# A layer with two attention stages: the softmax weighing moved to GpSimd alone, and the output projection's first weights loaded ahead

## The reference, cut to what matters

```
h = u @ w_in
o_nsa = nsa_mixer(q_a, ...)         # 8 heads of 64 in 2 groups: three branches, each softmax weighed by a gate
o_mla = mla_mixer(cq, ckv, k_rope)  # 8 heads of 96/64 on rms-normed latents of rank 384 and 256, causal over all keys
y = concatenate([o_nsa, o_mla]) @ w_out
x = layer_norm(ALPHA * x + (1 + g2) * y)
p = e / max(sum(e), 1e-30)          # in every softmax; e are the exponentials
```

## Time and profile before

| what | us |
|---|---|
| median of three runs (lowest, highest) | 2243.52 (2240.02, 2244.45) |
| the profiled execution, own time | 2248.16 |
| its span, first to last instruction | 2246.2 |
| PE, DVE, ACT, POOL busy in the span | 2093.4, 1543.6, 992.7, 707.0 |
| mean granted TensorE clock | 0.965 of full speed |

### The profile page before, as it was taken

The page is one execution under the profiler, slowest core; times in us unless marked ns, Lnnn a source line. Parts: engine busy times, 40 slices in busy tenths (PEclk is TensorE's granted clock), DMA queues, the critical chain, the costliest instruction groups (busy, mean ns, idle before and its releaser), DMA issues. The chain is left out here.

```text
span 2246.2 us, 28288 instructions
## 1 busy us (share of the span) xinstructions
PE 2093.4 (93%) x10025; PEld 1749.0 (78%) x10025; DVE 1543.6 (69%) x2387; ACT 992.7 (44%) x1901; POOL 707.0 (31%) x657
## 2 busy tenths in 40 slices
PE   6999999999999999788998889889899999999997
PEld 4888888878887887777786877767788888887885
DVE  6777777766887314798887487853765555558689
ACT  3433333334554123777876456530833333324443
POOL 0366555511100001255451032300245565640301
PEclk9999999999998999799998989989999999999999
DMA  7245555468831311300000000040333333247975
GB/s 266 94 162 168 169 169 169 159 206 261 244 105 62 123 45 43 87 1 1 1 1 1 1 1 1 1 145 18 133 117 104 112 106 120 93 125 264 295 258 100
DMA packets 193633, 254.39 MB, mean 113 GB/s; under 512 B 18192, under 2 KB 116560, under 8 KB 193495
## 3 DMA queue, kind: packets, MB, share of 16 engines
q1 hardware_dynamic: 178088, 208.04, 27.9%
q0 software_dynamic: 15408, 44.57, 7.6%
HBM read 212.72 MB, written 43.52 MB: 114 GB/s over the span
## 5 line engine op out<-in xcount | busy, mean ns | idle before, releaser
L2856 POOL TENSOR_TENSOR nsa_exps<-nsa_exps,nsaa_factor 128x512 f32<-128x512 f32 (+1 forms) x96 | 90.4, 972 | 120.5 <-DVE nsaa_factor L2836 120.5
L749 DVE TENSOR_TENSOR ffn2A_u<-ffn2A_u,ffn_banks 128x512 f32<-128x512 f32 x60 | 41.2, 687 | 117.4 <-PE ffn_banks L693 117.4
L1283 DVE SCALAR_TENSOR_TENSOR late_part_late<-ada_rows,far_silu_c,late_part_late 128x1024 f32<-128x1024 f32 x56 | 106.7, 1906 | 5.3 <-DMA ada_rows<-in_w_ada 5.3
L570 ACT ACTIVATE ffn1A_t_hi<-ffn1A_t 128x512 fp32r<-128x512 f32 x80 | 48.5, 628 | 132.6 <-POOL ffn1A_t L563 101.7
L570 ACT ACTIVATE ffn2A_t_hi<-ffn2A_t 128x512 fp32r<-128x512 f32 x80 | 48.4, 628 | 122.2 <-POOL ffn2A_t L563 91.3
L2783 ACT ACTIVATE nsaa_turned_hi<-nsaa_ring 128x512 fp32r<-128x512 f32 (+1 forms) x148 | 85.3, 599 | 35.0 <-PE nsaa_ring L2744 24.8
L2026 PE MATMUL in_acc<-mix_in_w_hi,mix_in_u_hi 128*128 128x494 f32 x256 | 99.2, 388 | 0.8 <-PEq L86 0.8
L2026 PE MATMUL in_acc<-mix_in_w_lo,mix_in_u_hi 128*128 128x494 f32 x256 | 99.2, 388 | 0.0
L2026 PE MATMUL in_acc<-mix_in_w_hi,mix_in_u_lo 128*128 128x494 f32 x256 | 99.2, 388 | 0.0
L2823 DVE TENSOR_TENSOR nsaa_turned_lo<-nsaa_ring,nsaa_turned_hi 128x512 fp32r<-128x512 f32 x132 | 87.9, 683 | 14.3 <-ACT nsaa_turned_hi L2783 12.3
L693 PE MATMUL ffn_banks<-ffn1S_s_hi,ffn1A_t_hi 128*128 128x512 f32 x240 | 93.8, 391 | 0.0
(11 more groups left out here) (640 smaller groups left out, 7035.3 us busy)
## 6 DMA issues: line engine op xcount, KB each, us to landing
ada_rows<-in_w_ada POOLq DMA_DIRECT2D x56, 512.0 KB, 4.7
ffn_raw_g<-in_ffn_wg SPq DMA_DIRECT2D x44, 512.0 KB, 3.7
ffn_raw_u<-in_ffn_wu SPq DMA_DIRECT2D x44, 512.0 KB, 5.0
early_w<-in_w_ada SPq DMA_DIRECT2D x16, 512.0 KB, 7.0
mix_in_w_raw<-in_w_in SPq DMA_DIRECT2D x32, 247.0 KB, 2.6
ffn_rest<-in_ffn_wd SPq DMA_DIRECT2D x29, 256.0 KB, 5.4
hidden<-ffn1A_c SPq DMA_DIRECT2D x22, 256.0 KB, 4.6
hidden<-ffn1A_u SPq DMA_DIRECT2D x22, 256.0 KB, 5.0
```

Source lines behind the costliest of these rows:

```text
L570: act.activation(self.b_hi[w][:, :], self.block_of(w), ACT.Copy).then_inc(self.rounded, 1)
L749: dve.tensor_tensor(out, base, bank, ALU.add).then_inc(self.mixed, 1)
L1283: dve.scalar_tensor_tensor(out=part_late[:, v, :], in0=ada[:, n % 2, :], scalar=silu_c[:, k:k + 1], in1=part_late[:, v, :], op0=ALU.mult, ...
L2856: pool.tensor_tensor(at, at, by, ALU.mult).then_inc(weighed_pool, 1)
```

## The change

- Weighing: POOL weighs all blocks in both stages; DVE's weigh step (L2841) is gone. A unit has no `by_vector` any more.
- `scale_latents` is done by POOL, after its last weigh step of each of the first 16 sparse units.
- The plan: `pool_price` falls from 2.9 to 1.67 a column (and 100 to 145 an instruction), with 1100 for a `scale_latents`; DVE's factor step is priced 300 throughout. In the latent stage PE's ranks for scoring, turning, applying change from (2, 0, 1) to (1, 0, 2).
- The output projection's gate row and first four chunks of w_out are asked for by SP inside the latent stage, as soon as PE is done with the last stage step. They go to the places of ukv_lo and ukv_hi; the chunks' high and low parts later go to the places of kv_hi and kv_lo. These four tiles are not read after the last stage step.

```diff
 def pool_price(u, step):
     kind, n, k = step
-    return 100 + (4 - u.weighed_rows(k)) * u.keys * 2.9
+    own = 145 + (4 - u.first_row(u.blocks[k])) * u.keys * 1.67
+    return own + (1100 if u.gate is not None and n < 2 * TT and k == len(u.blocks) - 1 else 0)
...
     streams = {"pe": [scoring, turning, applying], "act": [scores, filled, folding],
-               "dve": [scores, filled, factors, by_vector, folding], "pool": [by_pool]}
+               "dve": [scores, filled, factors, folding], "pool": [weighing]}
...
         @block.sync
         def _(sp):
             if ahead is not None:
                 ahead(sp)
+            if behind is not None:
+
+                sp.wait_ge(ring_full, max(m for x, m in ring_no.items() if x[0] == "stage") + 1)
+                behind(sp)
...
-                    if k < u.by_vector:
-                        pe.wait_ge(weighed_dve, weigh_no["weigh", n, 0] + 1)
-                    else:
-                        pe.wait_ge(weighed_pool, weigh_no["weigh", n, k] + 1)
+                    pe.wait_ge(weighed, weigh_no["weigh", n, k] + 1)
...
-                    if beside is not None:
-                        beside(dve, n)
                     dve.wait_ge(floored, n + 1)
                     dve.reciprocal(factor[:, b, :], floor[:, b, :]).then_inc(factored, 1)
-                elif kind == "weigh":
-                    dve.wait_ge(factored, n + 1)
-                    for r in range(4):
-                        at = u.room[:, r, 0:min(u.widths[r], u.by_vector * u.keys)]
-                        last = dve.tensor_scalar(at, at, factor[:, n % SUMS, r:r + 1], None, ALU.mult)
-                    last.then_inc(weighed_dve, 1)
...
-                pool.tensor_tensor(at, at, by, ALU.mult).then_inc(weighed_pool, 1)
+                pool.tensor_tensor(at, at, by, ALU.mult).then_inc(weighed, 1)
+                if beside is not None and k == len(u.blocks) - 1:
+                    beside(pool, n)
...
-               {"pe": (2, 0, 1), "act": (1, 0, 2), "dve": (2, 1, 0, 0, 3), "pool": (0,)}, 0)
+               {"pe": (1, 0, 2), "act": (1, 0, 2), "dve": (2, 1, 0, 3), "pool": (0,)}, 0, behind=behind)
```

More of the change, by code:

```diff
@@ L1833, in __init__ @@
         if gate_dram is not None:
-            self.gate = s.sb("gate", [P, w_dram.shape[1]])
+            self.gate = places[1] if places else s.sb("gate", [P, w_dram.shape[1]])
             self.gate_in = s.sem("gate_in")
@@ L1925, in load @@
                     chunks.load(sp, n, c)
-            if reload is not None:
-                chunks.ahead(sp)
             load(0, slots)
@@ L2434, in __init__ @@
         self.together = 4 if max(widths) <= T // 4 else 2 if max(widths) <= T // 2 else 1
-        self.by_vector, self.room = by_vector, room
-    def parts_weighed(self):
-        whole = [(0, self.by_vector)] if self.by_vector else []
-        return whole + [(k, k + 1) for k in range(self.by_vector, len(self.blocks))]
-    def weighed_with(self, k):
-        return 0 if k < self.by_vector else k
-    def weighed_rows(self, k):
-        return 0 if k < self.by_vector else self.first_row(self.blocks[k])
+        self.room = room
     def columns(self, row, width=None):
@@ L2527, in dve_price @@
     if kind == "factor":
-        return 300 if u.gate is None or n >= 2 * TT else 520
-    if kind == "weigh":
-        return 4 * (60 + u.by_vector * u.keys * 0.52)
+        return 300
     return (4 - u.first_row(u.blocks[k])) * P * 1.04 + 70 if kind == "turn" else 670
@@ L2557, in plan @@
         factors += [("factor", n, 0)]
-        for k0, k1 in u.parts_weighed():
-            (by_vector if k0 < u.by_vector else by_pool).append(("weigh", n, k0))
+        weighing += [("weigh", n, k) for k in range(len(u.blocks))]
         if u.closes:
@@ L2605, in needs @@
         elif kind == "turn":
-            found.append(("dve" if k < u.by_vector else "pool", ("weigh", n, u.weighed_with(k))))
+            found.append(("pool", ("weigh", n, k)))
         elif kind == "apply":
@@ L2639, in plan, with attend @@
     return order
-def attend(nc, stage, units, staging, folding, ident, ident_r, copies, first, slack, ahead=None, beside=None):
+def attend(nc, stage, units, staging, folding, ident, ident_r, copies, first, slack, ahead=None, beside=None, behind=None):
     order = plan(units, copies, first, slack)
@@ L2962, in sparse_attention, with latent_attention @@
         attend(nc, stage + "a", units, Staging(), Folding(), ident, ident_r, 6,
-               {"pe": (0, 1, 2), "act": (2, 0, 1), "dve": (2, 1, 0, 0, 3), "pool": (0,)}, 0, ahead=ahead, beside=scale_latents)
-def latent_attention(nc, stage, h, kv_hi, kv_lo, ukv_hi, ukv_lo, v, ident, ident_r, causal):
+               {"pe": (0, 1, 2), "act": (2, 0, 1), "dve": (2, 1, 0, 3), "pool": (0,)}, 0, ahead=ahead, beside=scale_latents)
+def latent_attention(nc, stage, h, kv_hi, kv_lo, ukv_hi, ukv_lo, v, ident, ident_r, causal, behind):
     with Scope(nc, stage) as s:
@@ L3030, in unit @@
                         lambda r: [((4 * half + r) * P, causal[:, :])], lambda j: v[:, head, j, :], 2 * head + half, True, True,
-                        None, before, 3, 1360, 3 * half, rooms[2 * b + half])
+                        None, before, 3, 1360, rooms[2 * b + half])
         class Folding:
@@ L3131, in layer @@
                                  compressed, rstd, latent_weights.ahead)
+            with Scope(nc, "out_w") as early:
+                early.sb("base", [P, 4 * T])
+                out_raw, out_gate = early.sb("raw", [P, Chunks.SLOTS, HALF]), early.sb("gate", [P, D])
+            split = h_alive.enter_context(Scope(nc, "split"))
+            kv_hi = split.sb("kv_hi", [P, 2, T], F32R)
+            kv_lo = split.sb("kv_lo", [P, 2, T], F32R)
+            ukv_hi = split.sb("ukv_hi", [P, 2, HEADS * P], F32R)
+            ukv_lo = split.sb("ukv_lo", [P, 2, HEADS * P], F32R)
+            slots_of = lambda at: at[:, :, :].rearrange("p a (b n) -> p (a b) n", n=HALF)
+            places = (out_raw, out_gate, slots_of(kv_hi), slots_of(kv_lo))
+            chunks = Chunks(split, w_out[0], HALF, gate_dram[0:1, :], places=places)
             with Scope(nc, "latent") as b:
[L3133 to L3136 removed]
                 v = b.sb("v", [P, HEADS, TT, P], F32R)
@@ L3143, in layer @@
                 latent_in.__exit__(None, None, None)
-                latent_attention(nc, "mla", h, kv_hi, kv_lo, ukv_hi, ukv_lo, v, ident, ident_r, causal)
+                latent_attention(nc, "mla", h, kv_hi, kv_lo, ukv_hi, ukv_lo, v, ident, ident_r, causal, chunks.ahead)
             clear_semaphores(nc)
@@ L3152, in layer @@
             x_back = r.sem("x_back")
-            chunks_in = Scope(nc, "w_out", side="right")
-            chunks_in.__enter__()
-            chunks = Chunks(chunks_in, w_out[0], HALF, gate_dram[0:1, :])
             heads_out = [COL_Q + c * P for c in range(HEADS // 2)] + LATENT_OUT
```

34 lines of the change are left out of this document (16 added, 18 removed).

## The result

The changed kernel takes 2204.35 us (median of 4 runs, 2200.80 to 2207.36), the kernel before 2243.98 us beside it (4 runs, 2240.02 to 2246.43). The ratio is 0.9824, with a 95% interval of 0.9802 to 0.9847: 39.6 us less. The profiled execution took 2202.52 us with a span of 2200.7 us, 45.6 us less than that of before; the mean granted clock is 0.977 (0.965 before).

A forecast was written before the change was run, and what follows sets the result against it. Latent attention was held bound by a chain of waits, chiefly PE's for DVE's weighing; DVE nearly bound part of the sparse stage. 24.5 + 5.7 + 4.8 = 35.0 us off the median 2243.5 gave 2208.5 us; range 2194 to 2230.

The forecast's parts named there:

- the likeliest case: Whole kernel: a time of 2200 to 2217 us, given a chance of 0.57.
- its largest term: Latent attention: 24.5 us saved, 20.3 over seven intervals between heads and 4.2 at the last half 1.
- The latent chain: Latent attention: PE's waits for DVE's weighing and the clock's falls behind them go; a head takes 20.9 us, not 23.8.
- The sum over heads: Latent attention: seven intervals between eight heads, each 2.9 us shorter, give 20.3 us.
- The last half 1: Latent attention's end: the wait of 5.3 us falls to POOL's 1.1 us, giving 4.2 us.
- The floor and the new waits: Latent attention, per head: PE's own work is the floor at 19.9 us, plus 1.0 us of new waits.
- the ring's turnaround: Latent attention: PE's new order waits for three banks and their copies; 1.3 us a turnaround, up to 2.5 us a head.
- The sparse attention: Sparse stage: 5.7 us from two thirds of DVE's 8.6 us relief, between 0 and 12; nothing for the reordering.
- POOL's scaling: Sparse stage: each scaling on POOL takes 0.8 us, between 0.37 and 1.5, covered by POOL's idle time.
- The projection: Output projection: early loads let PE start at 1474.3, not 1479.08, saving 4.8 us; range 4 to 7.5.
- The page on ports: Sparse stage: a shared SBUF port lets busier POOL hold DVE's small operations, 7 us; hence two thirds of 8.6 us.
- The last rival: Reordering gives nothing and POOL's late latents take the sparse gain: 4.8 us from the projection, 2238 us; chance 0.05.

The follow-up runs named there:

- experiment 1: Kernel before, with POOL weighing every block of the latent attention at its old price and PE's old rank; 2221.24 us, ratio 0.9905.
- Experiment 6: Kernel before, nothing moved, but POOL waits in the latent attention until DVE has weighed its blocks; 2213.01 us, ratio 0.9866.
- Experiment 2: Changed kernel with PE's rank in the latent attention as before, (2, 0, 1); 2211.36 us, ratio 0.9869.
- experiment 7: Kernel before with only PE's ranks in the latent attention changed to (1, 0, 2); 2244.62 us, ratio 1.0005.
- 8: Changed kernel, but its latent attention has the division, prices and rank of before, with POOL weighing behind DVE; 2201.65 us, ratio 0.9804.
- 9: As 8, with the new POOL price and rank (1, 0, 2) in the latent attention and the planner told of POOL's wait; 2200.22 us, ratio 0.9794.
- experiment 3: Changed kernel with the latents scaled by DVE again, prices of DVE and POOL as without it; 2205.41 us, ratio 0.9839.
- experiment 5: Changed kernel with POOL's steps at the old price in both attention stages; 2227.75 us, ratio 0.9926.
- experiment 4: Changed kernel with the gate row and first w_out chunks asked for at the projection again; 2206.68 us, ratio 0.9834.
- experiment 10: As 9, but DVE weighs all of the latent attention and POOL does nothing there; 2231.16 us, ratio 0.9938.

## Why the prediction was right

The forecast was 2208.5 us; 2204.35 was measured, inside both the range and the likeliest case's own. The mechanism of its largest term is the one that the chip shows. That the sum comes so close is in part luck: the two profiled executions lie 45.6 us apart where the steps gave 35.0, and only the medians lie 39.6 apart. By its own steps:

**The latent chain: right, its cause incomplete.** PE's wait for the weighing and the clock's falls behind it are gone, as experiment 1 shows by that edit alone. A head takes 20.7 us in the steady state; 20.9 was forecast. DVE's 15.9 us and POOL's 10.3 us a head were right within a microsecond: in the 20.85 us of one head from 1303.95 on they are busy for 16.7 and 9.5. But the prediction took DVE's 1058 ns as what the operation costs. Experiment 6 puts it at 415 ns: the other 643 ns are POOL's presence. The 4.0 us were a collision, and the change removes it by leaving one party.

**The sum over heads: mis-sized.** "Seven intervals of 2.9, 20.3 us" measured 27.1. The first gave 4.4 (it was 24.84 before, not 23.8), five gave 3.0 to 3.2, and the last gave 7.4. What shortens that one isn't shown: it is 14.03 us in experiment 1, with the old rank and price, but 17.20 in 2, 17.63 in 6 and 16.52 in 7. "The last half 1: 4.2" measured 1.65 (6.4 less the seam's 4.75), so the two together are 28.8 for 24.5.

**The floor and the new waits: right in sum, wrong in parts.** I had 19.9 us of PE's work and 1.0 us of waits from the ring's turnaround. The windows of after show 98.4% busy: 20.4 us of work and 0.3 of waits in 20.7. Experiment 2 shows that the turnaround is what the old rank pays. Why PE's work is 20.4 in the new order and 19.9 in the old one (experiments 6 and 8: PE full, 19.9 a head, 20.6 in 9 with the new order) is settled in part. Counted from one matmul's start to the next, less the waits, over four heads of each, it is 20.46 us a head in the changed kernel and 19.94 in experiment 6, and the applies of the blocks of 384 and 128 columns make the difference: 1.59 us a head for 1.05. Why PE goes on later behind them in the new order, where they stand among turned blocks, isn't known.

**The sparse attention: the step that failed in size.** "The new POOL price also reorders the stage; I give that nothing" was wrong. I forecast 5.7 us from DVE's relief and a stage of about 273; 9 to 13 us came (263.7 to 267.9 for 277), or 7 to 12 by the end of the last matmul (267.7 to 272.0 for 279.2). DVE's busy time over the whole stage is 5.5 us less (232.3 for 237.8), at the lower end of the forecast 5 to 9. The relief itself was about right, 6.0 to 6.6 us in the one profile that bears on it. What was missing is the reordering: experiment 3 leaves 6.5 us (4.8 to the last matmul) without any relief, and experiment 5, with the relief and the old price, loses 7 against the kernel before. What ties them, argued and not shown: the old price puts a block of 512 columns at 100 + 512 x 2.9 = 1585 ns, the new one at 1000, and POOL takes 1040, so the old plan puts PE's turns later than they could come.

**POOL's scaling: under-priced, and covered.** I took 0.8 us, between 0.37 and 1.5. It is 1.24 us for 384 columns and 0.92 for 256, slower than POOL's own two-operand product (825 and 612). PE waited for POOL in the whole stage twice, 0.9 us in all.

**The projection: right.** 4.8 us forecast, 4.75 measured, and 4.9 by experiment 4. The clock behind the start is 0.64 and not 0.50 over 6 us, which is most of the 1.1 us that the stage gives on top.

**The page on ports: cited for the wrong side.** The row first: DVE's weighing took 1058 ns beside POOL and 415 alone, with no other edit. In experiment 10, with POOL idle, it takes 0.52 ns a column ((748 - 278) / 896), half of what the same engine takes per column of a maximum from PSUM (1225 for 1024 columns, 292 for 128: 1.04 ns). The Trainium skill (Advanced Engine Details and Errata, VectorE Performance Modes) says that operations with source and destination in SBUF can run at two elements a cycle over two ports, one of them shared with GpSimd, and that the two engines' instructions then block each other; both rows agree, though no run here separates the port from another clash of the two in SBUF. I had used it only as a reason against a busier POOL, for DVE's small operations. They do still get held: the sparse floor operation, four columns, takes 151/164/1073 ns after (min, median, max), where before it took 150/163/868. But the large sufferer was the weighing itself, and by this rule the change was for the better: it leaves DVE no wide SBUF operation beside POOL's.

**The last rival** (2238 us, a chance of 0.05) counted only the projection's 4.8 us. It left out the latent attention's 24.5 without giving a reason; with them it would have stood at about 2214.

**The rest.** The 3.1 us more behind the projection are no effect of the change: both kernels issue the same instructions there, and two more profiles of the changed kernel take 676.9 and 678.0 us for 680.4, before 677.3. Why the two profiled executions lie 45.6 us apart and the medians 39.6 isn't explained: the profiled one of before is 4.2 us above its median, that of after 1.8 below, and it is one of those with the short low stretch in the sparse attention.

## What to carry to other kernels

Before moving work off an engine whose instructions look slow, find out what they cost alone: here one added wait, which keeps the two engines from weighing at the same time, gave 31 us by itself, where the whole change gave 40. Where a planner writes the order, its prices are part of the kernel; a moved step must be priced as measured, and an edit to rank or price is judged only together with the others. And a short wait of PE costs more than itself where the clock falls behind it, so a gain is counted in both.

## What the runs showed of the hardware

- A VectorE `tensor_scalar` on SBUF, 128x384 f32, takes 415 ns alone and 1058 ns in the mean beside GpSimd's `tensor_tensor` on SBUF; GpSimd's own 128x512 goes from 1039 to 1097 ns. VectorE pays nearly all of it.
- GpSimd's `tensor_scalar` with a factor per partition takes 1243 ns for 384 columns and 923 for 256, its `tensor_tensor` with the factor broadcast 825 and 612. The one-operand form is the slower one.
- In the kernel before, the granted clock was at its lower level for 3.4 us behind each of six waits of PE of 2.2 to 2.4 us, one in each head. Such a wait doesn't bring it every time: it fell behind four of seven waits of 2.4 to 2.5 us in experiment 7 and behind five of seven of 2.1 us in experiment 10. It did not fall behind waits of 1.2 us in experiment 2 and 1.5 us in experiment 5, one in a head and in every second head, nor in the steady heads of the changed kernel, where none is over 1.0 us. At the start of the sparse attention two profiles of the changed kernel differ with the same instructions: the clock stayed low for 13.7 us in one and 20.5 us in the other, and the stage took 263.7 and 267.9 us (with the order of before it took 277 with either). A difference of that size between two profiles needs a look at the clock first.
